# Order of the first loads, place of the first rounding, and the store in four parts, in a fourteen-stage transformer kernel

## The chip, the cores and the metric

The kernel runs on one core of a Trainium2 chip. The metric is the time of one execution on the device, in microseconds (us); of several runs the median counts.

## What is computed

Two transformer blocks one after the other, each two layers deep, on x of 256 positions by 1024 channels in float32. A layer is a feed-forward block, a mixer and a second feed-forward block; the second block of layers has a gated addition behind each layer. What matters here is the very first stage and the very last one:

```python
def rmsnorm(x, g):
    xf = x.astype(jnp.float32)
    y = xf * lax.rsqrt(jnp.mean(xf * xf, axis=-1, keepdims=True) + EPS)
    return (y * g.astype(jnp.float32)).astype(x.dtype)

def swiglu_ffn(x, w_gu, w_down):
    gate, up = jnp.split(x @ w_gu, 2, axis=-1)
    return (jax.nn.silu(gate) * up) @ w_down
...
        gate = jax.nn.sigmoid(rms_norm(x, ln_ple[i]) @ ple_w_gate[i])
        x = x + gate * (p[i] @ ple_w_in[i])
    return x
```

The first stage is x + 0.5 * swiglu_ffn(rmsnorm(x)), with 2816 hidden channels. The last stage is the gated addition at the end. All 360 MB of weights are read once.

## The kernel before, in words

x stays in SBUF for the whole run, as X (tile Xt): 128 positions in the partitions, i = 0, 1 for the two halves of the positions, 1024 channels in the row. n = 0, 1 are the halves of the channels; `in.x01` is the load of i = 0, n = 1.

Every product is made exact by splitting both sides into a rounded part and a remainder. ScalarE writes the rounded part (`hi`, L369, tile WH; for x `flip_act`, L519, tile XBt), VectorE subtracts it for the remainder (`lo`, L380, tile WL; for x `flip_dve`, L527, tile XBt). x is first turned by TensorE, in 128 x 128 blocks, into PSUM (`flip_pe`, L504, the transposes of L207), half a row of channels at a time; the rounding reads it from there. The scale of the norm is applied later, through sums of squares that ScalarE takes (`square` in `unscaled`, L546, tile work), a short chain on VectorE (tile small), and a row of scales that TensorE spreads.

A feed-forward stage (`ffn`, L655) walks over NFF = 22 pieces of weights, `f1.0.0` to `f1.0.21` in the first stage (the text calls them f1.0, f1.1, ... by their last number). A piece is 128 x 3072: part 0 gate, part 1 up, part 2 down, 512 KB each. TensorE multiplies gate and up of piece j, and the down part of piece j - 2. Pieces 0 and 1 (`NARROW`) use matmuls of 256 columns only, the later ones 512 and 256. In piece 0 the products of the first two channel groups (12 matmuls) come first, then the second half of x is turned (`norm.pe(P, 1)`), then the rest.

Each engine has its own program, written out stage by stage; an engine works strictly in the order of its program and waits on counters of the others. In the first stage ScalarE (`act`, L743) starts with

```python
hi(A, f"{t}.0", (0, 1))
norm.act(A)
hi(A, f"{t}.1", (0, 1))
```

that is, the weights of piece 0, then x, then piece 1; VectorE's `dve` has the same order.

The loads are issued by SyncE (`sync`, L2864), apart from three small tables on ScalarE's queue: the vectors (vt, 140.5 KB), rt and r4. First the first 256 columns of the constants (128 KB: the unit matrix for the turns and a matrix of ones), then x in four parts of 256 KB, then the weights in the order of `plan()` (L25) into a ring of three slots. A slot of 3072 columns has a front of 2048 and a rear of 1024; each is loaded again as soon as its remainders are made (`front[r]`, `rear[r]`, by `lo` of the piece three back). Behind the second piece the rest of the constants (ct, 1086.5 KB) is loaded, `if k == 1`, L2895. They are first used at piece 5 of the first stage (`params_dve`, L625, and `params_act`, L645), where also the parameters derived from rg_lambda are made.

The last stage (`ple`, L2763) adds to X in four steps, n outer and i inner, each two operations of VectorE; when the last is done SyncE stores all of X in one DMA and waits for it.

Of the kernel before, what the change touches and what calls it, by code (L numbers as in the profile page):

```python
# [10 lines left out]
ACT = mybir.ActivationFunctionType  # L11
# [236 lines left out]
def build(nc, wts, vecs, rows4, rowb, cons, rgw, xin, out):  # L248
    ctx = ExitStack()
    with ctx:  # L250
# [76 lines left out]
        def raw(name):  # L327
            a = AT[name] % NSLOT * SLOT
            return ring[:, a:a + COLS[name]]
# [216 lines left out]
        def unscaled(t, g, prev, rows, whole=False):  # L546
# [6 lines left out]

            def act(A, between=None):
                def square(half, i):
                    A.wait_ge(f"{prev}.x{i}{half}")
                    A.act(SQ4[:, half, i, :], X[:, i, half * 512:half * 512 + 512], ACT.Square,
                          accum_out=n_s4[:, 2 * half + i:2 * half + i + 1], inc=f"{t}.sq" if half and i else None)

                flip_act(A, t, g, 0)  # L560
                square(0, 0)
                square(0, 1)
                if between:
                    between(A)
                square(1, 0)
                flip_act(A, t, g, 1)
                square(1, 1)
# [57 lines left out]
        def params_dve(V, j):  # L625
            if j == 5:
                V.wait_ge("vt", "rt", "r4", "ct1")
                V.set(r0[:, :], 0.0)
                V.ts(hbr, vec("rg_b_r"), 0.5, None, MUL, None)
                V.ts(hbi, vec("rg_b_i"), 0.5, None, MUL, None)  # L630
                V.tt(gqk, vec("dsa_q_norm_2"), vec("dsa_k_norm_2"), MUL)
                V.ts(nl, vec("rg_lambda"), -1.0, None, MUL, None)
            if 6 <= j <= 8:
# [21 lines left out]
        def ffn(t, g, prev):  # L655
# [87 lines left out]
            def act(A):  # L743
                hi(A, f"{t}.0", (0, 1))
                norm.act(A)
                hi(A, f"{t}.1", (0, 1))
# [26 lines left out]

            def dve(V):
                lo(V, f"{t}.0", (0, 1))
                for q in range(0 if first else 1, 5):
                    norm.dve(V, q)
                    if q == 3:
                        lo(V, f"{t}.1", (0, 1))
# [2084 lines left out]
        def sync(S):  # L2864
            S.dma(ct[:, 0:256], cons[:, 0:256], "cons0", inc="ct0")
            for n in range(2):
                for i in range(2):
                    S.dma(X[:, i, n * 512:n * 512 + 512], xin[i * 128:i * 128 + 128, n * 512:n * 512 + 512], f"x{i}{n}", inc=f"in.x{i}{n}")
            at = 0
            front, rear = [()] * NSLOT, [()] * NSLOT  # L2870
            for k, (name, n, two) in enumerate(PL):
# [4 lines left out]
                if k == 0:  # L2876
                    for part in range(2):
                        s = slice(part * 1024, part * 1024 + 1024)
                        S.dma(raw(name)[:, s], src[:, s], f"first{part}", inc=f"{name}:ld{part}")
                    S.dma(raw(name)[:, 2048:n], src[:, 2048:n], "rear0", inc=f"{name}:ld")  # L2880
                elif n <= 2048:
# [11 lines left out]
                if n > 2048:  # L2893
                    rear[r] = [f"{name}:lo2"] if two else front[r]
                if k == 1:  # L2895
                    S.dma(ct[:, 256:], cons[:, 256:], "cons1", inc="ct1")
            S.wait_ge(*[f"pl1.x{i}1" for i in range(2)])
            S.dma(out.rearrange("a (i p) d -> p (a i) d", p=128), X, "outs", inc="out")
            S.wait_ge("out")

# [8 lines left out]
        def scalar(A):  # L2909
            A.dma(vt[:, :], vecs, "vecs", inc="vt")  # L2910
            A.dma(rt[:, :], rowb, "rowb", inc="rt")
            A.dma(r4[:, :], rows4, "rows4", inc="r4")
            A.wait_ge("ct0", "vt")
            for s in stages:
                s.act(A)
# [189 lines left out]
```

## Time and profile before

| | us |
|---|---|
| median of 3 runs (2261.34 to 2262.3) | 2261.38 |
| the profiled execution, its own time | 2263.45 |
| its span in the trace | 2261.6 |
| TensorE busy (PE) | 2178.2 (96%) |
| VectorE busy (DVE) | 1633.3 (72%) |
| ScalarE busy (ACT) | 1286.8 (57%) |
| GpSimd busy (POOL) | 91.5 (4%) |
| mean granted TensorE clock | 0.985 |
| read from HBM | 359.76 MB, 160 GB/s over the span |

The span is the part of the execution that the trace shows; 1.85 us of the execution's own time lie outside of it. Busy time of an engine says how much of the span it had an instruction running; what decides the end is the chain of waits, in which each piece of work is followed back to what released it. Times of a timeline row are from the start of the span. PE is TensorE, PEld its weight load, SPq the DMA issues of SyncE.

### The profile page before, as it was taken

How to read it: one execution, taken by the hardware profiler on the slowest of the kernel's cores; microseconds unless marked ns; L12 is line 12 of the kernel's file. 1: busy time of each engine (PE TensorE's matmuls, PEld its weight loads, DVE VectorE, ACT ScalarE, POOL GpSimd, SP SyncE). 2: the span in 40 equal slices, each digit the busy share in tenths (PEclk: the TensorE clock that was granted, in tenths of full speed). 3: DMA queues.
4: the chain of work that ended last, by engine and by line, in shares of the span. 5: the costliest groups of instructions: out<-in, count | busy, mean ns of one | idle time of the engine just before them, and what ended most of it. 6: DMA issues, size and time to landing. Idle time of an engine off the chain costs nothing.

```text
span 2261.6 us, 33574 instructions
## 1 busy us (share of the span) xinstructions
PE 2178.2 (96%) x12389; PEld 1861.8 (82%) x12389; DVE 1633.3 (72%) x2970; ACT 1286.8 (57%) x2142; POOL 91.5 (4%) x52
## 2 busy tenths in 40 slices
PE   7999989999999999999899989999999999989998
PEld 6888978888888966888688887888887888978886
DVE  6877778778777454877687765668776877868775
ACT  5655765555555265655465557455555655556553
POOL 0001000000003210000000000200001000000001
PEclk9999999999999999999899998999999999999999
DMA  6454345554553421455265441135544554435552
GB/s 246 185 194 146 138 159 196 191 183 176 185 188 143 170 103 57 159 194 183 108 224 189 141 152 65 39 121 196 194 178 157 190 188 164 150 120 188 187 195 80
DMA packets 64653, 362.99 MB, mean 160 GB/s; under 512 B 7464, under 2 KB 8232, under 8 KB 32488
## 3 DMA queue, kind: packets, MB, share of 16 engines
q1 hardware_dynamic: 64064, 360.31, 43.8%
q8 instruction: 97, 1.59, 0.3%
q14 instruction: 68, 0.56, 0.1%
q10 hardware_dynamic: 296, 0.27, 0.0%
q0 software_dynamic: 128, 0.26, 0.0%
HBM read 359.76 MB, written 1.05 MB: 160 GB/s over the span
## 4 chain that ended last, share of the span: by engine, by line
PE 81%; DVE 11%; ACT 5%; issue 1%; DMA 1%; POOL 0%; DVEq 0%; SPq 0%; ACTq 0%; POOLq 0%
PE ps L202 79%; DVE WL L120 5%; ACT work L192 2%; PE ps L207 2%; ACT WH L192 2%; DVE work L120 1%; DVE work L131 1%; ACT XBt L192 1%; DVE XBt L131 1%; DMA ring<-wts 1%; DVE small L131 1%; DVE small L120 1%; DVE Xt L131 0%; DVE work L157 0%; DVE work L125 0%
## 5 line engine op out<-in xcount | busy, mean ns | idle before, releaser
L202 PE MATMUL ps<-XBt,WH 128*128 128x512 f32 (+1 forms) x4208 | 1217.9, 356 | 23.1 <-DVE XBt L131 15.5
L120 DVE TENSOR_TENSOR WL<-ring,WH 128x1024 fp32r<-128x1024 f32 x636 | 783.6, 1232 | 292.8 <-ACT WH L192 244.6
L192 ACT ACTIVATE WH<-ring 128x1024 fp32r<-128x1024 f32 x664 | 703.6, 1060 | 364.4 <-PE ps L202 301.1
L202 PE MATMUL ps<-XBt,WL 128*128 128x256 f32 x3384 | 898.5, 281 | 0.0
L202 PEld LDWEIGHTS ps<-XBt,WH 128*128 128x128 f32 x4208 | 733.8, 191 | 131.1 <-DVE XBt L131 22.4
L202 PEld LDWEIGHTS ps<-XBt,WL 128*128 128x128 f32 x3384 | 644.4, 190 | 26.2
L202 PE MATMUL ps<-WH,HHt 128*128 128x512 f32 x712 | 280.5, 394 | 9.1 <-DVE WL L120 5.3
L202 PE MATMUL ps<-WL,HHt 128*128 128x512 f32 x712 | 278.5, 391 | 0.0
L202 PE MATMUL ps<-WH,HLt 128*128 128x512 f32 x712 | 275.8, 391 | 0.0
L192 ACT ACTIVATE work<-ps 128x256 f32<-128x256 f32 (+5 forms) x450 | 185.0, 414 | 74.9 <-PE ps L202 37.1
L192 ACT ACTIVATE work<-work 128x256 f32<-128x256 f32 (+6 forms) x222 | 99.2, 447 | 183.9 <-DVE work L120 179.6
L120 DVE TENSOR_TENSOR work<-ps,work 128x256 f32<-128x256 f32 (+3 forms) x376 | 166.1, 442 | 47.4 <-PE ps L202 9.1
L202 PE MATMUL ps<-WH,XBt 128*128 128x512 f32 (+3 forms) x528 | 168.3, 388 | 12.2 <-DVE WL L120 10.9
L192 ACT ACTIVATE HHt<-work 128x256 fp32r<-128x256 f32 (+1 forms) x185 | 76.1, 411 | 160.5 <-DVE work L120 160.5
L202 PE MATMUL ps<-work 128*128 128x128 f32 (+10 forms) x936 | 157.4, 318 | 10.3 <-ACT work L192 6.7
L202 PEld LDWEIGHTS ps<-WH,HHt 128*128 128x128 f32 x712 | 134.6, 189 | 32.3 <-DVE WL L120 5.5
L202 PEld LDWEIGHTS ps<-WH,HLt 128*128 128x128 f32 x712 | 134.5, 189 | 29.2
L202 PEld LDWEIGHTS ps<-WL,HHt 128*128 128x128 f32 x712 | 134.5, 189 | 28.4
L120 DVE TENSOR_TENSOR work<-work 128x256 f32<-128x256 f32 (+2 forms) x338 | 142.1, 421 | 14.1 <-ACT work L192 2.5
L202 PEld LDWEIGHTS ps<-work 128*128 128x128 f32 (+5 forms) x936 | 116.5, 180 | 40.6 <-issue 14.7
L120 POOL TENSOR_TENSOR WL<-ring,WH 128x1024 fp32r<-128x1024 f32 x28 | 67.2, 2400 | 2003.0 <-DVE HLt L120 1426.0
L202 PEld LDWEIGHTS ps<-WH,XBt 128*128 128x128 f32 x528 | 99.1, 191 | 35.9 <-DVE WL L120 11.7
(132 smaller groups left out, 1263.1 us busy)
## 6 DMA issues: line engine op xcount, KB each, us to landing
ring<-wts SPq DMA_DIRECT2D x248, 1024.0 KB, 5.8
ring<-wts SPq DMA_DIRECT2D x180, 512.0 KB, 3.8
ring<-wts SPq DMA_DIRECT2D x1, 1152.0 KB, 5.0
ct<-cons SPq DMA_DIRECT2D x1, 1086.5 KB, 12.3
Xt<-x SPq DMA_DIRECT2D x4, 256.0 KB, 4.8
out<-Xt SPq DMA_DIRECT2D x1, 1024.0 KB, 4.0
ring<-wts SPq DMA_DIRECT2D x2, 256.0 KB, 2.6
ring<-wts SPq DMA_DIRECT2D x1, 288.0 KB, 4.5
```

The costliest lines, as they stand in the source:

```text
L120: self.done(self.e and self.e.tensor_tensor(out, a, b, op), inc)
L131: self.done(self.e and self.e.scalar_tensor_tensor(out, a, s, b, op0, op1), inc)
L192: self.done(self.e and self.e.activation(out, a, f, **kw), inc)
L202: inst = self.e and self.e.matmul(out, l, r, start=start, stop=stop)
L207: inst = self.e and self.e.transpose(out, a, ident)
```

## The change

Four things are edited. The second half of x (n = 1) is loaded behind the first two parts of the first weight piece and no longer in front of them, and the rest of the constants behind the fourth piece, no longer behind the second. ScalarE and VectorE round the first half of x before the first weight piece, in the first stage alone. ScalarE takes over the negation of rg_lambda (`nl`) from VectorE, as its first instruction, so that its function table is loaded there. And the result is stored in four parts of 256 KB, each as soon as it is added. No arithmetic is changed.

```diff
--- before.py
+++ after.py
@@ -551,13 +551,15 @@
             def pe(P, half):
                 flip_pe(P, t, X, half, lambda i, half: f"{prev}.x{i}{half}")
 
-            def act(A, between=None):
+            def act(A, between=None, early=None):
                 def square(half, i):
                     A.wait_ge(f"{prev}.x{i}{half}")
                     A.act(SQ4[:, half, i, :], X[:, i, half * 512:half * 512 + 512], ACT.Square,
                           accum_out=n_s4[:, 2 * half + i:2 * half + i + 1], inc=f"{t}.sq" if half and i else None)
 
                 flip_act(A, t, g, 0)
+                if early:
+                    early(A)
                 square(0, 0)
                 square(0, 1)
                 if between:
@@ -624,12 +626,11 @@
 
         def params_dve(V, j):
             if j == 5:
-                V.wait_ge("vt", "rt", "r4", "ct1")
+                V.wait_ge("vt", "rt", "r4", "ct1", "par.nl")
                 V.set(r0[:, :], 0.0)
                 V.ts(hbr, vec("rg_b_r"), 0.5, None, MUL, None)
                 V.ts(hbi, vec("rg_b_i"), 0.5, None, MUL, None)
                 V.tt(gqk, vec("dsa_q_norm_2"), vec("dsa_k_norm_2"), MUL)
-                V.ts(nl, vec("rg_lambda"), -1.0, None, MUL, None)
             if 6 <= j <= 8:
                 softplus_dve(V, "par", j - 6, c4, nl, tA, tB, tC)
             if j == 8:
@@ -741,8 +742,11 @@
                     ps.give(f"{t}.acc{i}1", f"{t}.x{i}1")
 
             def act(A):
-                hi(A, f"{t}.0", (0, 1))
-                norm.act(A)
+                if first:
+                    norm.act(A, early=lambda A: hi(A, f"{t}.0", (0, 1)))
+                else:
+                    hi(A, f"{t}.0", (0, 1))
+                    norm.act(A)
                 hi(A, f"{t}.1", (0, 1))
                 for j in range(NFF):
                     nx2, b = ahead(f"{t}.{j}"), j % 2
@@ -772,8 +776,10 @@
                         params_act(A, j)
 
             def dve(V):
+                for q in range(2 if first else 0):
+                    norm.dve(V, q)
                 lo(V, f"{t}.0", (0, 1))
-                for q in range(0 if first else 1, 5):
+                for q in range(2 if first else 1, 5):
                     norm.dve(V, q)
                     if q == 3:
                         lo(V, f"{t}.1", (0, 1))
@@ -2863,9 +2869,11 @@
 
         def sync(S):
             S.dma(ct[:, 0:256], cons[:, 0:256], "cons0", inc="ct0")
-            for n in range(2):
+            def x_in(n):
                 for i in range(2):
                     S.dma(X[:, i, n * 512:n * 512 + 512], xin[i * 128:i * 128 + 128, n * 512:n * 512 + 512], f"x{i}{n}", inc=f"in.x{i}{n}")
+
+            x_in(0)
             at = 0
             front, rear = [()] * NSLOT, [()] * NSLOT
             for k, (name, n, two) in enumerate(PL):
@@ -2877,6 +2885,7 @@
                     for part in range(2):
                         s = slice(part * 1024, part * 1024 + 1024)
                         S.dma(raw(name)[:, s], src[:, s], f"first{part}", inc=f"{name}:ld{part}")
+                    x_in(1)
                     S.dma(raw(name)[:, 2048:n], src[:, 2048:n], "rear0", inc=f"{name}:ld")
                 elif n <= 2048:
                     S.dma(raw(name), src, f"slot{r}", inc=f"{name}:ld")
@@ -2892,11 +2901,15 @@
                     front[r].append("od_wi")
                 if n > 2048:
                     rear[r] = [f"{name}:lo2"] if two else front[r]
-                if k == 1:
+                if k == 3:
                     S.dma(ct[:, 256:], cons[:, 256:], "cons1", inc="ct1")
-            S.wait_ge(*[f"pl1.x{i}1" for i in range(2)])
-            S.dma(out.rearrange("a (i p) d -> p (a i) d", p=128), X, "outs", inc="out")
-            S.wait_ge("out")
+            o3 = out.rearrange("a (i p) d -> p (a i) d", p=128)
+            for n in range(2):
+                for i in range(2):
+                    s = slice(n * 512, n * 512 + 512)
+                    S.wait_ge(f"pl1.x{i}{n}")
+                    S.dma(o3[:, i, s], X[:, i, s], f"outs{i}{n}", inc=f"out{i}{n}")
+            S.wait_ge("out00", "out10", "out01", "out11")
 
         def tensor(P):
             P.wait_ge("ct0", "vt")
@@ -2911,6 +2924,7 @@
             A.dma(rt[:, :], rowb, "rowb", inc="rt")
             A.dma(r4[:, :], rows4, "rows4", inc="r4")
             A.wait_ge("ct0", "vt")
+            A.act(nl, vec("rg_lambda"), ACT.Copy, scale=-1.0, inc="par.nl")
             for s in stages:
                 s.act(A)
 
```

**SyncE's queue, at the start of the program.** Each row is a DMA issue, target <- source. Before:

```order
L195 DMA ct<-cons 128x256
L195 DMA Xt<-x 128x512 x4
L195 DMA ring<-wts 128x1024 x3
L195 DMA ring<-wts 128x2048
L195 DMA ring<-wts 128x1024
L195 DMA ct<-cons 128x2173
L195 DMA ring<-wts 128x2048
L195 DMA ring<-wts 128x1024
L195 DMA ring<-wts 128x2048 [waits vector_done]
L195 DMA ring<-wts 128x1024 [waits vector_done]
```

After:

```order
L195 DMA ct<-cons 128x256
L195 DMA Xt<-x 128x512 x2
L195 DMA ring<-wts 128x1024 x2
L195 DMA Xt<-x 128x512 x2
L195 DMA ring<-wts 128x1024
L195 DMA ring<-wts 128x2048
L195 DMA ring<-wts 128x1024
L195 DMA ring<-wts 128x2048
L195 DMA ring<-wts 128x1024
L195 DMA ring<-wts 128x2048 [waits vector_done]
L195 DMA ring<-wts 128x1024 [waits vector_done]
L195 DMA ct<-cons 128x2173
```

Two x parts now stand behind two weight parts; the large load of constants has moved from behind the second piece to behind the fourth, whose rear part, the row ahead of it, waits for a counter of VectorE (the remainders of the first piece's down part).

**ScalarE, its first instructions.** WH is the rounded weight, XBt the rounded x, first0 and first1 the loads of the first two weight parts, vecs and cons0 those of the vectors and the first constants. Before:

```order
L192 ACT_TABLE_LOAD [waits first0,vecs]
L192 ACTIVATE WH<-ring 128x1024 [waits cons0]
L192 ACTIVATE WH<-ring 128x1024 [waits scalar_done,first1]
L192 ACTIVATE XBt<-ps,vt 128x256 [waits scalar_done,matmul_done]
L192 ACTIVATE XBt<-ps,vt 128x256
L192 ACTIVATE XBt<-ps,vt 128x256 [waits scalar_done,matmul_done]
L192 ACTIVATE XBt<-ps,vt 128x256 [waits scalar_done]
L192 ACTIVATE work,small<-Xt 128x512 [waits scalar_done,x00]
```

After:

```order
L192 ACT_TABLE_LOAD [waits vecs]
L192 ACTIVATE small<-vt 128x4 [waits cons0]
L192 ACTIVATE XBt<-ps,vt 128x256 [waits scalar_done,matmul_done]
L192 ACTIVATE XBt<-ps,vt 128x256
L192 ACTIVATE XBt<-ps,vt 128x256 [waits scalar_done,matmul_done]
L192 ACTIVATE XBt<-ps,vt 128x256 [waits scalar_done]
L192 ACTIVATE WH<-ring 128x1024 [waits scalar_done,first0]
L192 ACTIVATE WH<-ring 128x1024 [waits scalar_done,first1]
L192 ACTIVATE work,small<-Xt 128x512 [waits scalar_done,x00]
```

The table load waits for the vectors only; the four roundings of x stand in front of the two of weights, and only the first weight rounding waits for first0.

**VectorE, its first instructions** (the piece of the difference, - before, + after):

```order
-L2954 UNCONDITIONAL_BRANCH
-L120 TENSOR_TENSOR WL<-ring,WH 128x1024 x2
-L131 SCALAR_TENSOR_TENSOR XBt<-ps,vt,XBt 128x256 x8
+L2968 UNCONDITIONAL_BRANCH
+L131 SCALAR_TENSOR_TENSOR XBt<-ps,vt,XBt 128x256 x4
+L120 TENSOR_TENSOR WL<-ring,WH 128x1024 x2
+L131 SCALAR_TENSOR_TENSOR XBt<-ps,vt,XBt 128x256 x4
 L120 TENSOR_TENSOR WL<-ring,WH 128x1024 x2
 L120 TENSOR_TENSOR small<-small 128x2
```

The four remainders of the first half of x now stand in front of the two of the first weight piece; the second half's four stay behind them.

## Rows read from the trace of the kernel before

**Rows 1.** The page, part 4: shares of the chain that ended last

```profile
PE 81%; DVE 11%; ACT 5%; issue 1%; DMA 1%; POOL 0%; DVEq 0%; SPq 0%; ACTq 0%; POOLq 0%
```

**Rows 2.** Timeline, 0 to 34 us: start us, us, engine and group [idle before <-releaser]

```profile
5.75 1.94 PE L207 MATMUL ps<-ct,Xt 128*128 128x128 f32 x8 [5.75 <-DMA Xt<-x]
9.41 1.28 ACT L192 ACT_TABLE_LOAD   x1 [9.41 <-DMA ring<-wts]
10.71 2.21 ACT L192 ACTIVATE WH<-ring 128x1024 fp32r<-128x1024 f32 x2
11.90 2.56 DVE L120 TENSOR_TENSOR WL<-ring,WH 128x1024 fp32r<-128x1024 f32 x2 [11.90 <-ACT WH L192]
13.01 1.57 ACT L192 ACTIVATE XBt<-ps,vt 128x256 fp32r<-128x256 f32 x4
14.58 1.85 DVE L131 SCALAR_TENSOR_TENSOR XBt<-ps,vt,XBt 128x256 fp32r<-128x256 f32 x4
15.60 0.76 PE L202 MATMUL ps<-XBt,WH 128*128 128x256 f32 x2 [7.90 <-DVE XBt L131]
18.29 1.91 PE L207 MATMUL ps<-ct,Xt 128*128 128x128 f32 x8
19.81 1.57 ACT L192 ACTIVATE XBt<-ps,vt 128x256 fp32r<-128x256 f32 x4 [2.79 <-PE ps L207]
20.69 1.86 DVE L131 SCALAR_TENSOR_TENSOR XBt<-ps,vt,XBt 128x256 fp32r<-128x256 f32 x4 [4.26 <-ACT XBt L192]
22.29 4.48 ACT L192 ACTIVATE WH<-ring 128x1024 fp32r<-128x1024 f32 x4
```

**Rows 3.** DMA issues, 1.1 to 3.3 us: KB each, median us from issue to landing

```profile
vt<-vecs ACTq DMA_DIRECT2D x1, 140.5 KB, 3.1
...
ring<-wts SPq DMA_DIRECT2D x1, 512.0 KB, 6.2
Xt<-x SPq DMA_DIRECT2D x1, 256.0 KB, 5.3
```

**Rows 4.** By stretch: PE, PEld, DVE, ACT, POOL busy (x), clock, DMA share, GB/s

```profile
15.60:18.00 2.40, 2.40 (x11) 2.40 (x12) 0.83 (x2) 1.33 (x4) 0.00 (x0) 1.00 1.02 426
25.00:31.00 6.00, 6.00 (x50) 5.84 (x48) 5.31 (x18) 1.68 (x2) 0.00 (x0) 1.00 0.01 3
...
50.00:100.00 50.00, 50.00 (x267) 42.88 (x266) 40.36 (x71) 32.21 (x48) 0.00 (x0) 1.00 0.54 202
```

**Rows 5.** Chain that ended last, 30 to 80 us: start us, us, what

```profile
34.94 45.08 PE ps L202 x238
```

**Rows 6.** DMA issues of three stretches, 6.3 to 39 us

```profile
ring<-wts SPq DMA_DIRECT2D x1, 1024.0 KB, 14.3
...
ring<-wts SPq DMA_DIRECT2D x1, 512.0 KB, 3.6
...
ring<-wts SPq DMA_DIRECT2D x1, 1024.0 KB, 5.7
```

**Rows 7.** Timeline of SP and ACT, 33 to 43 us

```profile
34.36 69.22 SPq L195 DMA_DIRECT2D ring<-wts  x20
...
41.08 1.06 ACT L192 ACTIVATE WH<-ring 128x1024 fp32r<-128x1024 f32 x1
42.95 0.42 ACT L192 ACTIVATE work<-work 128x256 f32<-128x256 f32 x1 [0.81 <-DVE work L120]
```

**Rows 8.** Timeline of DVE and SP, 2256 to 2262 us

```profile
2256.42 0.69 DVE L131 SCALAR_TENSOR_TENSOR Xt<-work,Xt 128x512 f32<-128x512 f32 x1
2257.19 0.40 SPq L195 DMA_DIRECT2D out<-Xt  x1
```

**Rows 9.** DMA, 2257 to 2262 us: GB/s in 40 slices, and the issue

```profile
GB/s 0 0 0 0 0 0 0 0 164 328 459 393 459 328 426 393 426 459 328 492 328 459 328 459 360 426 360 426 393 197 0 0 0 0 0 0 0 0 0 0
out<-Xt SPq DMA_DIRECT2D x1, 1024.0 KB, 4.0
```

**Rows 10.** DMA issues of 2200 to 2240 us

```profile
ring<-wts SPq DMA_DIRECT2D x1, 256.0 KB, 2.6
```

## The prediction

> **What bounds the kernel now.** I read the chain of waits first. Over the whole run it is TensorE for 81%, and DMA for 1% [rows 1]: loads bind only where nothing has been computed yet, and at the very end. So a change of the load order can act in two places, and between them it can only pass a shift on.
>
> *The head.* The timeline from 0 to 34 us [rows 2] is to be read as a list of what TensorE lacks. It turns the first half of x as soon as that has landed (5.75 us, eight transposes) and then stands idle for 7.90 us, until the first product at 15.60. What it lacks is made by ScalarE, in program order. ScalarE waits for the first weight part until 9.41, loads its table (1.28), rounds two parts of weights (from 10.71), and only then rounds x (from 13.01), although the turned x had lain in PSUM since 7.7. VectorE's remainders follow, the one of x last (14.58), and TensorE starts 1.02 us after that one begins.
>
> *The tail.* The last addition ends at 2257.11, and SyncE issues the store of the whole result at 2257.19 [rows 8]; it lands 4.0 us later, 1.05 MB at 328 to 492 GB/s with about 0.9 us before the first byte and 0.45 us behind the last [rows 9]. The span ends 0.4 us after that.
>
> **The change, part by part.** *Landing times first.* The loads stand on one queue and land in that order, each as the bytes ahead of it allow. The last of the four x pieces, issued at about 2.61, landed 5.3 us later, at 7.9; the first weight part, issued at 3.08, landed 6.2 later, at 9.3 [rows 3]. Each pair of x pieces is 512 KB, as is one weight part. After the change the first weight part has exactly as many bytes ahead as that last x piece had, so it lands at 7.9; at worst it stays at 9.3. The second half of x now lands where the second weight part did, one further 512 KB on, by about 10.9. The first half of x keeps its place behind the first constants, so TensorE's transposes stay at 5.75.
>
> *ScalarE's table.* The load goes with the small copy of rg_lambda, which waits for the vectors; they land 3.1 us after an issue at 0.7 [rows 3], at 3.8. The table is in by 3.8 + 1.28 + 0.2 for the copy = 5.3, and the first work for ScalarE is there at 7.27 (next step): nothing, hidden by 2 us of waiting for x. The copy replaces a VectorE operation on 4 columns at piece f1.5, where VectorE has room: nothing either.
>
> *The first product.* The second turn of x gives the spacing: transposes from 18.29, ScalarE's rounding from 19.81, so 1.52 later, 1.57 for the four roundings; VectorE 0.88 behind them, 1.86 long [rows 2]. Laid on 5.75: ScalarE rounds x from 7.27 to 8.84, VectorE has x's remainders by 10.01. ScalarE's first weight rounding starts at 8.93, the weights having been there for 1.0 us; VectorE's remainder of it started 1.19 behind (10.71 to 11.90), so at 10.12, and takes 1.23 (half of 2.56 less the gap), to 11.36. With the 0.14 us from a remainder's end to the product, TensorE starts at 11.5 in place of 15.60: **-4.1 us**. The second weight part's remainder ends at about 12.7, and six products of 0.22 us [rows 4] keep TensorE until 12.8, so no new wait. If the weights land at 9.3 instead, all of this moves by 0.45: that bound gives -3.65. The other bound is -4.6, with the x pieces landing half a microsecond sooner since less is queued behind them.
>
> *Does the shift get through?* TensorE's next need is the second half of x, which it turns 2.69 us after its first product (15.60 to 18.29): now at 14.2, landed at 10.9, 3.3 us of cover. ScalarE by then must have done its three squares, formerly 2.4 us from 14.67; now they start at 11.1 and end at 13.6, before the turned second half at 15.7. From there both engines do the same work in the same order, and all is passed on. Piece f1.1, rounded from 22.29 [rows 2], has the same bytes ahead as before. Piece f1.2 landed 14.3 us after its issue at 6.48, at 20.8 [rows 6]; it is needed by the third of the four roundings from 22.29, at 24.5, now 20.4, so it would be 0.4 late, but the 1.1 MB of constants no longer stands ahead, which is worth 2.7 us at the store's rate [rows 9].
>
> *The constants' new place* is behind the last third of f1.3, whose issue waits for a buffer, at 34.36 [rows 7], now 30.3. Nobody needs them before the sixth piece, some five pieces of 8.2 us (267 matmuls in 50 us, 44 to a piece [rows 4]) after 11.5: no wait there. But f1.4's load comes right behind. It was issued near 34.8 and landed 5.7 later [rows 6], at 40.5; ScalarE took it at 41.08. Now it would land at 40.5 - 4.1 + 2.7 = 39.1 and is wanted at 37.0. ScalarE stands 2.1 us, of which its own 0.81 of idleness takes a part [rows 7], and VectorE gets the next gate some 1.3 us late. TensorE works without a wait for 45 us from 34.94 [rows 5] at 8.2 us a piece and wants f1.4 first at 34.94 + 2 x 8.2 = 51.3, now 47.2; rounding and remainder end by 43. It wants piece 2's hidden values later still. So **0**, with 4 us of cover; without it, up to +2.1.
>
> *The store in quarters.* Three quarters go out while the last additions run and are on the way to the end before the fourth is issued at the same point as before, since each needs about 2 us and the additions are 1.7 us apart. What stays exposed is 256 KB. By the slices of the store [rows 9] that is 0.9 + 0.65 + 0.45 = 2.0 us, and by the nearest whole row, a load of 256 KB that had the queue nearly for itself, 2.6 [rows 10]. I take 2.3 between them: **-1.7 us**, bounds -2.0 and -1.4. The Trainium skill ("DMA: Bandwidth & Descriptors", Bandwidth) speaks against this: it asks for batches of 1 MiB or more, and by its anatomy (about 2.0 us fixed plus the bytes at 436 GB/s) a quarter would cost 2.6 us and the whole 4.4. Four quarters one behind the other would then be 10.4, but only the last is exposed, so by that page the tail is worth 1.8; this trace has 4.0 for the whole.
>
> *Sum:* -4.1 - 1.7 = -5.8 us. The profiled execution took 2263.45 us with a span of 2261.6, so that would be 2257.65 and 2255.8; against the median of the runs, 2261.38, it is **2255.6 us**. About 0.2%, or 4.5 us, is what a measurement can tell from no change.
>
> **The rivals.** *The late loads reach TensorE.* ScalarE and VectorE are in one order, and a stall in f1.4 or f1.2 could be handed on. For: both margins shrink, and the f1.4 one is gone (-2.1). Against: TensorE has no wait on record there for 45 us. Price 0.8 to 2.1 us: 2256.4 to 2257.7.
>
> *The head gives less.* If x and weights landed by another rule than the bytes ahead (the first half of x later, the second weight part not before 10.9), TensorE would start near 14, a gain of 1.6, and with the tail 3.3: 2258.1. Against: the two landings of [rows 3] differ by 1.4 us, what 512 KB take.
>
> *TensorE's clock, for the worse.* From 15.60 on its 256-column products take 0.22 us each, after 25 us 0.12 [rows 4]: the lower and the higher of 1.2 and 2.4 GHz, although the granted clock reads 1.00 in both. It rose after some 5 us of work without a gap. If, after the shorter idle stretch, it stayed low through the narrow pieces f1.0 and f1.1, some 80 products would cost 0.10 us more each: +8, and the kernel would be at 2263.6, slower. It decides once more than 58 extra products run low. Against: work is as dense as before, and nothing in the first 35 us makes it sparser.
>
> *The clock, for the better.* The transposes at 5.75 now lie only 3.8 us ahead; if the clock were high from the first product, twelve products and eight transposes would save up to 2.3 us: 2253.3.
>
> *The order doesn't matter* (the head's gain is eaten by a wait further on, such as the norm's chain on VectorE that is on the path from 25 to 34 us): only the tail, 2259.7. Against: that chain starts with the second turn of x, which moves as well.
>
> **How the numbers follow.** Forecast as summed 0.70 (2254.5 to 2256.6, from the bounds); late loads 0.10; less in the head 0.06; clock better 0.06; tail alone 0.05; slower by the clock or another new wait 0.03. The range from 2253.8 to 2257.8 leaves out the last three and part of the third. Faster than 2256.9: the forecast, the better clock and a third of the late loads, 0.80; within 0.2%: 0.17; slower 0.03.
>
> **What would show it.** In the profile after: the table load before 5.5 us; ScalarE's x roundings from 7.3, its weight roundings from 8.9; the first product at 11.5 with an idle stretch of 3.8 us; the second turn at 14.2; the long TensorE chain from 30.8; the last quarter landing 2.0 to 2.6 us after an issue 4.1 us earlier than 2257.19. A first weight landing after 9, a TensorE wait between 31 and 50 us, or products still at 0.22 us beyond 18 us would prove steps wrong.

## The result, and the profile after

| | before | after |
|---|---|---|
| median of 20 runs each, us | 2262.16 (2260.42 to 2267.07) | 2257.32 (2255.80 to 2261.55) |
| the profiled execution, its own time | 2263.45 | 2255.81 |
| its span | 2261.6 | 2254.0 |
| first product of TensorE | 15.60 | 11.17 |
| start of the long TensorE chain | 34.94 | 30.57 |
| end of the last addition to end of span | 4.5 | 2.5 |

The ratio of after to before is 0.9975, with a 95% interval of 0.9969 to 0.9981: 5.7 us less (0.0025 x 2262.16), between 4.3 and 7.0. The forecast was 5.8 less. The two medians by themselves are 4.8 apart, the two means 5.5, so the runs don't fix the gain to better than a microsecond. With more runs than the three known ahead, the scatter of both kernels is wider than it looked, some 6 us from the lowest to the highest; the section on the clock below shows where it is.

The timeline of all engines, 0 to 36 us, of the kernel after (start us, us, engine and group, [idle before <- what ended it]), and TensorE's first product below it, answers to [rows 2]:

```profile
3.84 1.28 ACT L192 ACT_TABLE_LOAD   x1 [3.84 <-DMA vt<-vecs]
5.38 1.95 PE L207 MATMUL ps<-ct,Xt 128*128 128x128 f32 x8 [5.38 <-DMA Xt<-x]
6.93 1.57 ACT L192 ACTIVATE XBt<-ps,vt 128x256 fp32r<-128x256 f32 x4 [1.60 <-PE ps L207]
8.60 2.20 ACT L192 ACTIVATE WH<-ring 128x1024 fp32r<-128x1024 f32 x2
9.88 2.56 DVE L120 TENSOR_TENSOR WL<-ring,WH 128x1024 fp32r<-128x1024 f32 x2
...
13.94 1.91 PE L207 MATMUL ps<-ct,Xt 128*128 128x128 f32 x8
15.46 1.57 ACT L192 ACTIVATE XBt<-ps,vt 128x256 fp32r<-128x256 f32 x4 [2.22 <-PE ps L207]
17.94 4.48 ACT L192 ACTIVATE WH<-ring 128x1024 fp32r<-128x1024 f32 x4
11.17 0.80 PE L202 MATMUL ps<-XBt,WH 128*128 128x256 f32 x2 [3.84 <-DVE WL L120]
```

The table load now lies in front of everything, at 3.84. ScalarE rounds x (6.93), then the weights (8.60), with no wait for a load between them; VectorE's remainder of the weights starts at 9.88 and TensorE's first product at 11.17, 3.84 us of idleness in place of 7.90. The rest of the ladder (second turn of x 13.94, its rounding 15.46, the four weight roundings 17.94) has the spacing of before, 4.35 us earlier.

The DMA issues of 2.0 to 2.3 us (first weight part) and of 3.6 to 4.1 us (last part of x), KB each and us from issue to landing, answer to [rows 3]:

```profile
ring<-wts SPq DMA_DIRECT2D x1, 512.0 KB, 5.6
...
Xt<-x SPq DMA_DIRECT2D x1, 256.0 KB, 6.8
```

The weight part, issued at 2.12, landed at 7.7, where the fourth part of x had landed before (7.9). The last part of x landed near 10.4.

The chain that ended last, 0 to 80 us, and ScalarE and VectorE from 36 to 41 us, answer to [rows 5] and [rows 7]:

```profile
30.57 49.46 PE ps L202 x260
```

```profile
38.68 1.06 ACT L192 ACTIVATE WH<-ring 128x1024 fp32r<-128x1024 f32 x1 [2.06 <-DMA ring<-wts]
40.15 0.42 ACT L192 ACTIVATE work<-work 128x256 f32<-128x256 f32 x1 [0.41 <-ACT WH L192]
...
39.77 1.22 DVE L120 TENSOR_TENSOR WL<-ring,WH 128x1024 fp32r<-128x1024 f32 x1 [1.23 <-ACT WH L192]
```

ScalarE waits 2.06 us for piece f1.4, behind the constants, and VectorE 1.23 us behind it; TensorE's chain from 30.57 on has no break.

The same two additions of VectorE near the end of the first stage, before and then after (timeline of VectorE, 203 to 208 us and 198.5 to 204 us):

```profile
205.75 1.41 DVE L131 SCALAR_TENSOR_TENSOR Xt<-ps,small,Xt 128x512 f32<-128x512 f32 x2
...
201.38 1.41 DVE L131 SCALAR_TENSOR_TENSOR Xt<-ps,small,Xt 128x512 f32<-128x512 f32 x2
```

They are 4.37 us apart, exactly what the starts of the long chain are (34.94 and 30.57). So the shift goes through the whole first stage, and f1.4's wait takes nothing of it.

The end: SyncE's stores and the last addition, then the DMA from 2246 us on (GB/s in 40 slices of 0.2 us), answer to [rows 8, 9]:

```profile
2246.36 5.48 SPq L195 DMA_DIRECT2D out<-Xt  x4
2250.79 0.69 DVE L131 SCALAR_TENSOR_TENSOR Xt<-work,Xt 128x512 f32<-128x512 f32 x1
...
GB/s 0 0 0 0 0 0 379 348 420 164 0 0 0 0 133 410 369 358 41 0 0 0 0 328 379 379 226 0 0 0 0 82 420 369 369 72 0 0 0 0
out<-Xt SPq DMA_DIRECT2D x4, 256.0 KB, 2.0
```

Four bursts of 0.65 us or so, each over before the next begins. A quarter lands 2.0 us after its issue. The last addition ends at 2251.48, 5.63 us earlier than before, and the span 2.5 us after that.

### The profile page after: what moved, and what is told of

Read it like the earlier page. It is cut to its first block, busy times and chain, and to the rows that moved or that the text cites. A ratio compares the mean times of both kernels' runs of the same rounds, so it can differ in the third digit from the quotient of the medians.

```text
span 2254.0 us, 33578 instructions
## 1 busy us (share of the span) xinstructions
PE 2180.0 (97%) x12389; PEld 1862.3 (83%) x12389; DVE 1633.0 (72%) x2969; ACT 1286.6 (57%) x2143; POOL 91.6 (4%) x52
## 4 chain that ended last, share of the span: by engine, by line
PE 79%; DVE 13%; ACT 5%; issue 1%; DMA 1%; POOL 0%; DVEq 0%; ACTq 0%; SPq 0%; POOLq 0%
PE ps L202 77%; DVE WL L120 5%; ACT work L192 3%; PE ps L207 2%; DVE work L120 1%; ACT WH L192 1%; DVE work L131 1%; ACT XBt L192 1%; DVE XBt L131 1%; DVE small L131 1%; DVE small L120 1%; DMA ring<-wts 0%; DVE Xt L131 0%; DVE work L125 0%; DVE work L157 0%
```

## The experiments

Each is the changed kernel with one edit (the last two rows of the table have two and three), and its time is compared with the kernel before. The profile figures are of one execution each. The total times scatter by more than most edits are worth, so each edit is read from the profile at three places: the first product, the start of the long chain, and the way from the last addition to the end. The column "between" is from the start of the long chain to the end of the last addition, where no edit can act but the extra loads and, at its last microseconds, the halved quarter. Where the long chain is in brackets, it has a break further on, for f1.4.

| kernel | ratio to before (95%) | first x rounding | first product | long chain | between | end |
|---|---|---|---|---|---|---|
| before | 1 | 13.01 | 15.60 | 34.94 | 2222.2 | 4.5 |
| changed | 0.9975 (0.9969 to 0.9981) | 6.93 | 11.17 | 30.57 | 2220.9 | 2.5 |
| one store | 0.9981 (0.9972 to 0.999) | 7.20 | 11.43 | 30.54 | 2221.0 | 4.5 |
| old rounding order | 0.9983 (0.9974 to 0.9992) | 10.11 | 12.54 | 31.57 | 2223.3 | 2.5 |
| all of x first | 0.9973 (0.9964 to 0.9982) | 7.71 | 12.06 | 31.08 | 2220.8 | 2.6 |
| constants early | 0.9972 (0.9961 to 0.9982) | 7.88 | 12.11 | 31.12 | 2218.1 | 2.5 |
| late table | 0.9985 (0.9976 to 0.9994) | 8.16 | 12.39 | 31.29 | 2220.6 | 2.5 |
| three extra loads | 1.0009 (1.0 to 1.0018) | 6.96 | 11.18 | (30.20) | 2230.8 | 2.5 |
| one extra load | 0.9978 (0.9968 to 0.9987) | 7.35 | 11.58 | (30.99) | 2221.4 | 2.5 |
| late small tables | 0.9973 (0.9963 to 0.9983) | 7.05 | 11.28 | 30.67 | 2224.1 | 2.6 |
| split rounding | one run, 2254.38 us | 6.78 | 10.08 | 29.42 | 2220.6 | 2.5 |
| split, late tables | 0.9968 (0.9955 to 0.998) | 6.67 | 9.97 | 29.37 | 2220.8 | 2.5 |
| the same, last quarter halved | 0.9963 (0.9951 to 0.9976) | 6.58 | 10.23 | 29.25 | 2223.5 | 2.2 |

**One store.**

```diff
-            for n in range(2):
-                for i in range(2):
...
-                    S.dma(o3[:, i, s], X[:, i, s], f"outs{i}{n}", inc=f"out{i}{n}")
+            S.wait_ge(*[f"pl1.x{i}1" for i in range(2)])
+            S.dma(o3, X, "outs", inc="out")
```

> The changed kernel with the result again stored in one DMA. Theory (the store's exposed part is set by the bytes of the last DMA): the time from the end of the last addition to the end of the span goes back from 2.52 us to the 4.49 of before, so 2.0 us more than the changed kernel; everything ahead of it as there, the long TensorE chain from 30.6 us. Rival (the end costs a fixed time whatever the size, the gain lay in the middle of the run): the end stays at 2.5 us.

The end is 4.5 us again (last addition 2251.57, span 2256.1), and the long chain starts where it did, at 30.54. So the four stores are worth 2.0 us, by the bytes of the last one. Shown.

**The old rounding order.** ScalarE and VectorE take the weights first again.

```diff
-                if first:
-                    norm.act(A, early=lambda A: hi(A, f"{t}.0", (0, 1)))
-                else:
-                    hi(A, f"{t}.0", (0, 1))
-                    norm.act(A)
+                hi(A, f"{t}.0", (0, 1))
+                norm.act(A)
```

> The changed kernel, but ScalarE and VectorE round the first weight parts ahead of x again; the order of the loads and the early table stay. Theory (ScalarE's order is part of the path): the weight rounding starts when the first part lands, 7.7 to 7.8 us, and the first product 4.89 us later, as before, at 12.7 in place of 11.17; the long TensorE chain starts at 32.1 in place of 30.57, 1.5 us more. Rival (the weights' landing was all that mattered): first product at 11.2, long chain at 30.6.

ScalarE (first two rows) and TensorE (last two) of this kernel, in the timeline:

```profile
7.65 1.06 ACT L192 ACTIVATE WH<-ring 128x1024 fp32r<-128x1024 f32 x1 [2.44 <-DMA ring<-wts]
10.11 1.57 ACT L192 ACTIVATE XBt<-ps,vt 128x256 fp32r<-128x256 f32 x4
...
12.54 0.77 PE L202 MATMUL ps<-XBt,WH 128*128 128x256 f32 x2 [5.34 <-DVE XBt L131]
31.57 0.47 PE L202 MATMUL ps<-XBt,WH 128*128 128x512 f32 x1 [0.59 <-DVE work L120]
```

ScalarE waits 2.44 us for the weights, for the last 0.8 us of it with turned x ready beside it; the first product comes 1.37 us after the changed kernel's, the long chain 1.0 us. The order of rounding carries that much. The loads and the table carry the rest: against the kernel before, the weights land 1.76 us sooner (7.65, not 9.41) and the table load of 1.28 us is out of the way, together 3.04, and the first product is 3.06 us earlier than before's 15.60. The long chain was expected at 32.1. It came 0.5 us sooner because the second turn of x took 1.40 us and not 1.91: TensorE's clock had risen by then.

**All of x ahead of the weights.**

```diff
             x_in(0)
+            x_in(1)
...
-                    x_in(1)
```

> The changed kernel, but the second half of x is loaded ahead of the weights again. Theory (landing by the bytes ahead): the first weight part lands 1.3 us later, at about 9.0 in place of 7.7, but ScalarE is busy with x until 8.6 anyway, so its weight rounding starts at 9.1 and the first product comes at 11.6 in place of 11.17, 0.45 us more. Rival (the new load order carries most of the gain): 1.4 us more or above.

ScalarE's first weight rounding, and below it TensorE's turn of the second positions and its first product:

```profile
9.69 1.06 ACT L192 ACTIVATE WH<-ring 128x1024 fp32r<-128x1024 f32 x1 [0.41 <-DMA ring<-wts]
...
6.98 1.12 PE L207 MATMUL ps<-ct,Xt 128*128 128x128 f32 x4 [0.50 <-DMA Xt<-x]
12.06 0.80 PE L202 MATMUL ps<-XBt,WH 128*128 128x256 f32 x2 [3.96 <-DVE WL L120]
```

The weights are there at 9.69, 2.0 us later than in the changed kernel and 0.7 later than expected, and ScalarE waits for them by 0.41 us. First product 0.89 us later, long chain 0.51: twice the 0.45 that was expected, and short of the rival's 1.4. TensorE also waited 0.50 us in the middle of the first turn for the second part of x, which has the same place in both kernels. That wait is not on the way to the first product, since ScalarE was through with x and still stood for the weights. Whether whatever held up that part of x held up the weights too, one execution doesn't tell.

**The constants back behind the second piece.**

```diff
-                if k == 3:
+                if k == 1:
```

> The changed kernel, but the rest of the constants is loaded behind the second piece again. Theory (both late loads lie in slack): ScalarE's wait of 2.06 us for piece f1.4 is gone, f1.2 lands near 20.5 with ScalarE wanting it at 20.1, the remainder is made at 24.6 all the same, the long TensorE chain starts at 30.57 and the time does not change. Rival A: the late f1.2 delays the norm's chain by 0.4 us or more. Rival B: the wait for f1.4 cost the changed kernel time, up to 2 us, which comes back here.

ScalarE's roundings of f1.2:

```profile
21.19 2.21 ACT L192 ACTIVATE WH<-ring 128x1024 fp32r<-128x1024 f32 x2 [0.55 <-DMA ring<-wts]
```

It waited 0.55 us for f1.2 (0.4 was expected), and not at all for f1.4. From the first rounding of x to the long chain it took 23.24 us, in the changed kernel 23.64: no loss (the 0.4 us less are the clock's: the second turn of x took 1.30 us, not 1.91). The head of this execution was 0.95 us late, which hid as much of the wait. Without that ScalarE would have stood up to 1.5 us, and it would still not have mattered: VectorE takes the remainder of f1.2 behind the norm's chain, at 25.12, 2.9 us after its gate part is rounded. Neither rival holds: both late loads lie in slack, and the constants' new place is worth nothing. That its first product is late (12.11) comes from the second part of x, which let TensorE wait 1.02 us in the first turn.

**The table loaded late.** The copy is left out of ScalarE's program and VectorE negates rg_lambda.

```diff
-            A.act(nl, vec("rg_lambda"), ACT.Copy, scale=-1.0, inc="par.nl")
...
+                V.ts(nl, vec("rg_lambda"), -1.0, None, MUL, None)
```

> The changed kernel without the early copy of rg_lambda on ScalarE (VectorE negates it again), so that the function table is loaded when ScalarE's first rounding of x is ready to run. Theory (the table load was hidden under the wait for x and is on the path without that): the table load starts at about 6.9, the rounding of x 1.3 us later at 8.2, the first product 1.3 us later relative to the transposes, the long TensorE chain at 31.9 in place of 30.57. Rival (the weights' landing covers it): no more than 0.3 us.

ScalarE's first rows, and TensorE's second turn:

```profile
6.86 1.28 ACT L192 ACT_TABLE_LOAD   x1 [6.86 <-PE ps L207]
8.16 1.57 ACT L192 ACTIVATE XBt<-ps,vt 128x256 fp32r<-128x256 f32 x4
...
15.17 1.19 PE L207 MATMUL ps<-ct,Xt 128*128 128x128 f32 x8
```

The 1.28 us stand in the path, and the first product is 1.22 us later than in the changed kernel. The long chain is only 0.72 later: the second turn of x ran in 1.19 us where the changed kernel took 1.91, so TensorE's clock had already risen. That this gives back part of a delay ahead of the first product is not shown: the kernel with three extra loads had its first product at 11.18, as the changed kernel, and its second turn took 1.32 us all the same, with the long chain at 30.20. From the first product to the long chain the thirteen kernels need 18.9 to 19.1 us or 19.3 to 19.4, by when the clock rises.

**Extra loads ahead of f1.4**, three of 1 MB, then one:

```diff
                     S.dma(ct[:, 256:], cons[:, 256:], "cons1", inc="ct1")
+                    S.dma(work[:, 10000:12048], wts[0:128 * 2048].rearrange("(p n) -> p n", p=128), "spare0", inc="spare0")
```

> The changed kernel with three more loads of 1 MB, into an unused place of the tile work, behind the constants and so ahead of piece f1.4. Nothing is computed from them; the parameters' step at piece 5 waits for them. At 2.6 us per MB, f1.4 lands 7.9 us later, at 46.5, ScalarE waits 10 us for it in place of 2.06. Theory (4 us of cover between the changed kernel's f1.4 and TensorE): the cover is used up, TensorE, which wants f1.4 at 30.57 + 2 x 8.2 = 47.0, waits 2 to 4 us there and the time grows by that. Rival (ScalarE's wait is passed on from the start): 8 us. Rival (cover larger than thought): nothing.

The chain that ended last, 28 to 120 us, with three extra loads:

```profile
31.91 14.54 DMA ring<-wts
46.47 1.06 ACT WH L192
47.56 1.24 DVE WL L120
48.84 71.37 PE ps L202 x369
```

The load of f1.4 is now a link of the chain, and the long chain begins anew at 48.84, after 4.58 us without work. By stretch (PE, PEld, DVE, ACT, POOL, granted clock, DMA share, GB/s):

```profile
48.80:52.00 3.20, 3.16 (x10) 2.77 (x11) 2.64 (x5) 2.36 (x4) 0.00 (x0) 0.50 0.13 22
52.00:55.00 3.00, 3.00 (x17) 2.56 (x17) 2.65 (x5) 2.02 (x4) 0.00 (x0) 0.99 0.94 365
```

After the stall the granted clock is 0.50 for 3.2 us, so the stall should cost about 1.6 us more than it lasts. It does: VectorE's two additions near the end of the first stage start at 207.37, where the changed kernel has 201.38, and with the long chain's start 0.37 us earlier here that is 6.4 us for stall and low clock. The expectation, 2 to 4 us, was too small. The time between is 2230.8, 9.9 us over the changed kernel's, and the ratio says 7.7 us; what is left of the 9.9 is within what the column "between" scatters for other kernels. It also shows where TensorE wanted f1.4: at 48.84 - 4.58 = 44.26, 14.06 us after the start of the long chain, not two pieces of 8.2 after it. The chain begins in the middle of piece 2, with the up part.

> The changed kernel with one more load of 1 MB ahead of piece f1.4. f1.4 lands 2.6 us later, ScalarE waits 4.7 us. With three such loads TensorE wanted the piece at 14.06 us behind the start of the long chain; here its remainder would be done at 41.0 + 2.6 = 43.6, 1.0 us before 44.6. Theory (cover of 3.6 us in the changed kernel): no wait of TensorE, long chain unbroken, no change of the time against the changed kernel. Rival (any wait of ScalarE is passed on): 2.6 us more and a TensorE wait before 50 us.

TensorE's one wait between 31 and 60 us:

```profile
48.27 0.50 PE L202 MATMUL ps<-XBt,WH 128*128 128x512 f32 x1 [0.36 <-DVE WL L120]
```

ScalarE waited 4.54 us, TensorE 0.36, and that for the up part of f1.4, whose remainder is made 4.3 us after the gate part's. No wait was expected. By the end of the first stage (202.51 against 201.38, less the 0.42 us that the long chain began later) it has cost 0.7 us. The changed kernel's row for the same remainder (timeline of VectorE, 44 to 46 us):

```profile
44.09 1.23 DVE L120 TENSOR_TENSOR WL<-ring,WH 128x1024 fp32r<-128x1024 f32 x1
```

It is made at 45.32, and the product that takes it starts at 47.32 there. So the changed kernel's f1.4 has 2.0 us of cover, by the up part; the 4 us of the forecast and the 3.6 of this expectation looked at the gate part only.

**The small tables issued late.**

```diff
-            A.dma(rt[:, :], rowb, "rowb", inc="rt")
-            A.dma(r4[:, :], rows4, "rows4", inc="r4")
             A.wait_ge("ct0", "vt")
             A.act(nl, vec("rg_lambda"), ACT.Copy, scale=-1.0, inc="par.nl")
+            A.dma(rt[:, :], rowb, "rowb", inc="rt")
+            A.dma(r4[:, :], rows4, "rows4", inc="r4")
```

> The changed kernel with the two small tables on ScalarE's queue (120 KB and 64 B, not needed before piece 5) issued after the early copy, so they no longer share the engines with x. Theory (x lands by the bytes in flight ahead of it): 0.12 MB less, both quarters of x 0.3 to 0.4 us earlier, ScalarE's rounding of x at 6.6 in place of 6.9 to 7.9, the first product 0.3 us earlier or more. Rival (x's landing has a fixed part only): no change beyond the scatter.

TensorE's first turn of x, in two parts:

```profile
4.72 1.09 PE L207 MATMUL ps<-ct,Xt 128*128 128x128 f32 x4 [4.72 <-DMA Xt<-x]
6.32 1.12 PE L207 MATMUL ps<-ct,Xt 128*128 128x128 f32 x4 [0.51 <-DMA Xt<-x]
```

The first part of x came at 4.72 (5.0 to 5.4 in the kernels without the edit), the second not before 6.32, and ScalarE needs both. First product 11.28, long chain 30.67: nothing gained in this execution. The expectation fell for the second part. Where the second part held up TensorE in kernels without the edit, it came at 6.5 to 7.2. The two kernels further down that also have the edit began to round x at 6.67 and 6.58, those without it at 6.78 to 7.88 (the old order and the late table left aside), so a few tenths of a microsecond may be there; it stays open.

**The rounding of x split**, alone and with the late tables:

```diff
-                flip_act(A, t, g, 0)
-                if early:
-                    early(A)
+                if early:
+                    flip_one(A, 0)
+                    early(A)
+                    flip_one(A, 1)
+                else:
+                    flip_act(A, t, g, 0)
```

> The changed kernel with only the split rounding of x (first quarter, the two weight parts, second quarter), the small tables back in their place. Theory: where the x landings are as in the changed kernel, ScalarE's weight rounding waits for neither x nor weights beyond 7.8 us; first product 0.7 us earlier than with the whole half ahead, near 10.4 to 10.6. Rival (the gain of the kernel with both edits was all from the tables): 11.2.

> As the kernel with late small tables, and ScalarE and VectorE round only the first quarter of x's channel groups ahead of the first weight parts, the second quarter behind them (the first 12 products need no more). Theory: x's first rounding 6.6 to 7.4, weights landed at 7.4, their rounding at 7.5 in place of 8.60, remainder at 8.75, first product near 10.1 in place of 11.17, the long TensorE chain near 29.5: 1.1 us less than the changed kernel, about 6.7 less than before. Rival (the second quarter now comes late for the products behind the second turn): TensorE waits there and the long chain starts at 30.3 or later.

The timeline of the kernel with the split alone, ScalarE, then TensorE:

```profile
6.78 0.84 ACT L192 ACTIVATE XBt<-ps,vt 128x256 fp32r<-128x256 f32 x2 [1.28 <-PE ps L207]
7.71 1.06 ACT L192 ACTIVATE WH<-ring 128x1024 fp32r<-128x1024 f32 x1
...
10.08 0.80 PE L202 MATMUL ps<-XBt,WH 128*128 128x256 f32 x2 [2.91 <-DVE WL L120]
29.42 0.47 PE L202 MATMUL ps<-XBt,WH 128*128 128x512 f32 x1 [0.59 <-DVE work L120]
```

The weight rounding starts at 7.71, about as the weights land, and the first product comes at 10.08, 1.1 us earlier than in the changed kernel; the long chain at 29.42. With the late tables it is 9.97 and 29.37. So the gain is the split's, and the rival about the tables is out. That kernel's median is 2255.17 us, ratio 0.9968; the interval overlaps with the changed kernel's, and only the profile's 1.2 us separate the two.

**The last quarter in two halves of 256 columns**, on top of both:

```diff
+                            for c in range(2):
+                                s = slice(c * 256, c * 256 + 256)
...
+                                V.stt(T2[:, s], TH[:, n, i, s], 1.0, ps[f"{t}.half{c}"][:, 0:256], ADD, MUL, inc=f"{t}.pieh{c}")
+                                V.stt(xv[:, s], T2[:, s], 0.5, xv[:, s], MUL, ADD, inc=f"{t}.x11" if c else f"{t}.x11a")
```

> The kernel with late tables and split rounding, and at the end the last quarter of the result computed, added and stored in two halves of 256 columns. Theory (the exposed end is the last addition pair and the last store's bytes): two additions of 0.43 in place of 0.70 us behind the last matmul, 0.5 us less, and 128 KB in place of 256 KB, 0.3 us less at 410 GB/s: from the last matmul's end to the end of the span 0.8 us less, the landing at 1.7 in place of 2.0. Rival (a fixed part rules the store): 0.5 us only.

Its last matmuls, VectorE's four steps, and the last two stores:

```profile
2244.00 7.04 PE L202 MATMUL ps<-ring 128*128 128x512 f32 x20
2250.89 0.42 DVE L131 SCALAR_TENSOR_TENSOR work<-work,ps 128x256 f32<-128x256 f32 x1
2251.35 0.42 DVE L131 SCALAR_TENSOR_TENSOR Xt<-work,Xt 128x256 f32<-128x256 f32 x1
2251.88 0.42 DVE L131 SCALAR_TENSOR_TENSOR work<-work,ps 128x256 f32<-128x256 f32 x1
2252.33 0.42 DVE L131 SCALAR_TENSOR_TENSOR Xt<-work,Xt 128x256 f32<-128x256 f32 x1
...
out<-Xt SPq DMA_DIRECT2D x2, 128.0 KB, 1.7
```

The store lands 1.7 us after its issue, as expected. But the four short steps, 0.42 us each, stand one behind the other on VectorE, and the second pair starts at 2251.88, 0.8 us after TensorE's last matmul ended (2244.00 + 7.04 = 2251.04). From the start of the last matmul group to the end of the span it is 2255.0 - 2244.00 = 11.0 us. In the changed kernel the same group starts here:

```profile
2243.00 7.03 PE L202 MATMUL ps<-ring 128*128 128x512 f32 x16
```

and the span ends at 2254.0, so 11.0 us too. The 0.3 us of the store are spent on the additions. No gain.

## The clock, and the scatter of the runs

The column "between" goes from 2218.1 to 2224.1 us for kernels whose code there is the same. Two of them have the same granted clock, within 0.01, in every stretch of 10 us but two, those from 1410 and from 1990 us. The stretch 1410 to 1420 us of the kernel with all of x first, then of the one with early constants (columns as above), each followed by the same remainder of VectorE behind it (timeline of VectorE, 1402 to 1425 us):

```profile
1410.00:1420.00 10.00, 8.96 (x50) 8.48 (x51) 5.37 (x19) 4.71 (x12) 4.18 (x4) 0.66 0.01 2
...
1421.64 1.23 DVE L120 TENSOR_TENSOR WL<-ring,WH 128x1024 fp32r<-128x1024 f32 x1
```

```profile
1410.00:1420.00 10.00, 8.80 (x68) 7.92 (x68) 7.96 (x21) 4.72 (x12) 4.34 (x4) 1.00 0.01 2
...
1418.90 1.23 DVE L120 TENSOR_TENSOR WL<-ring,WH 128x1024 fp32r<-128x1024 f32 x1
```

In the first the clock was at 0.66 of full for 10 us, which is two thirds of the stretch at 1.2 GHz and, for an engine that never waits, 3.4 us of work lost; in the second it stayed up. At 1410.67 and 1410.82 us the two kernels are at the same addition of VectorE; at the remainder shown the second is 2.74 us ahead. So the stretch cost 2.9 us, and that is the whole difference between them (2220.8 - 2218.1 = 2.7). The stretch from 1990 us, at 0.66 against 1.00 too, cost nothing: behind it the second is 2.61 us ahead (2008.41 against 2011.02), as much as in front of it. Both stretches are in mixer stages, where TensorE stands still for others: 0.8 to 1.6 us at a time for ScalarE's and GpSimd's work around 1410, 2.8 and 0.8 us for ScalarE's around 1990. Of the 7.6 us between the spans of before and after, head (4.37) and end (1.97) make 6.34; the other 1.3 lie between. They are not there yet at 205 us, where the shift is 4.37 to the hundredth, and are of the size of this scatter, as is the difference between the 6.34 of the profiles and the 5.7 of the ratio. Whether the earlier start of everything makes the low stretches rarer was not tried; the kernels with the shifted start lie on both sides of before's 2222.2.

## Why the prediction was right

*The number.* 5.8 us less was forecast, and the ratio says 5.7, the landmarks 6.3. That the first agrees to 0.1 us is luck, with an interval of 4.3 to 7.0. As an absolute time the forecast was 2255.6, and 2257.32 came: inside the range, but above the 2254.5 to 2256.6 that "forecast as summed" stood for, and above the 2256.9 that it was to stay under with 0.80. 0.8 us of that is the kernel before, whose median is 2262.16 over twenty runs and was 2261.38 over three. (The bounds of the two terms add up to 2254.8 and 2256.3, not to the 2254.5 and 2256.6 given.) What carries the claim that the mechanism was right is the steps below.

*First product.* 4.1 us earlier was forecast, 4.43 came. ScalarE's rounding of x was put at 7.27 and began at 6.93, because x landed 0.37 us earlier than before; the step "TensorE's transposes stay at 5.75" was the one that was off, and its bound of half a microsecond took that in. All spacings held: 1.55 us from turn to rounding (1.52), 1.28 from weight rounding to remainder (1.19; VectorE was at x until then), 1.29 from there to the product.

*Landing by the bytes ahead.* The first weight part landed at 7.7 (7.9 forecast); the last part of x at 10.4 (10.9). What is equal for the first weight part after and the last x piece before are the bytes up to and with the load itself, not those ahead of it as the prediction says; the landing, 7.7 against 7.9, fits the former. With all of x in front the weights land at 9.69, so the new order of loads takes 2.0 us off their landing, of which 0.9 reach the first product and 0.5 the long chain (there the second turn took 1.31 us, not 1.91). The rival that the head gives less is out with that. The rule fails for a part of x alone: the second one, at the same place in the queue, came late enough to stall the turn, by 0.16 to 1.02 us, in six of the twelve profiled kernels that load the first half of x first.

*Table load.* Hidden as forecast, and worth 1.2 us at the first product when it is not.

*The shift gets through.* The second turn came at 13.94 (14.2), f1.2 was no limit, and the long chain moved by 4.37. At 205 us, behind the first stage, the shift was still 4.37. Further on it can't be told from the scatter of the clock.

*The constants' place.* ScalarE's wait for f1.4 was put at 2.1 us and was 2.06; its cost of 0 was right. The cover was mis-sized: 2.0 us in place of 4, since the long chain starts inside piece 2 and the up part's remainder is the later one. The reason for the move, though, is not there in the runs: with the constants early nothing is lost.

*The store.* -1.7 was forecast, with 2.3 us for a quarter between 2.0 and 2.6. It is 2.0, and the gain 1.97. The load of 256 KB was the wrong neighbour; the slices of the store itself gave the right number. By the Trainium skill ("DMA: Bandwidth & Descriptors", Anatomy of one DMA) a quarter is estimated at 2.6 us and the saving at 1.8; the page gives its figures for transfers that GpSimd issues, and these are issued by SyncE. The trace has 2.0 and 1.97. The advice of the same page (Bandwidth) to batch to 1 MiB is for the share of peak bandwidth. It is not what counts for this store at the end, where only the last transfer's time is exposed.

*The rivals.* Late loads that reach TensorE take one extra megabyte to begin. The clock was not high from the first product, whose neighbours still started 0.21 us apart, and it didn't stay low in the head: it rose during the second turn of x or just behind it, sooner in some executions than in others, which moved the long chain by up to 0.5 us. The tail alone is out, by the old rounding and late table kernels.

## What to carry to other kernels

In a kernel bound by one engine for 80% of its path, the start is a ladder of its own: list what the engine's first instruction lacks, in the order in which it arrives, and let each helper engine take first what lands first, its table load included. At the other end only the last store counts, so what is stored earlier is free, and splitting further pays only where the work ahead of the store does not grow. Edits worth a few microseconds of 2260 should be read from landmarks in the trace, because the clock in far stages moves the total by more.

## What the runs showed beside that

- A wait of TensorE can cost more than it lasts: 4.58 us of stall were followed by 3.2 us at a granted clock of 0.50 and cost 6.4 us in all.
- The same low clock (0.66 over 10 us) cost 2.9 us in one mixer stage and nothing in another.
- A 256 KB store of 2 KB rows lands 2.0 us after its issue, 128 KB of 1 KB rows 1.7, and 1 MB in one piece 4.0.
- At the start, products of 256 columns take 0.22 us with a granted clock of 1.00 in the record; later, 0.12. There the record of the clock doesn't show the lower level, the durations do.
